# Peer retrieval step: decoding the top 16 indices on 16-bit pairs with a tree of additions, one-hot products from expert 51 on, gathers laid out anew

## What is computed

```python
q = (xt @ w_query).reshape(n, PEER_HEADS, 2, PEER_KEY_DIM).astype(jnp.float32)
s = jnp.einsum('nhpd,hpkd->nhpk', q, sub_keys.astype(jnp.float32))
s1, i1 = lax.top_k(s[:, :, 0], PEER_TOPK)
s2, i2 = lax.top_k(s[:, :, 1], PEER_TOPK)
cand = (s1[..., :, None] + s2[..., None, :]).reshape(n, PEER_HEADS, PEER_TOPK * PEER_TOPK)
cidx = (i1[..., :, None] * N_KEYS + i2[..., None, :]).reshape(n, PEER_HEADS, PEER_TOPK * PEER_TOPK)
top, pos = lax.top_k(cand, PEER_TOPK)
eidx = jnp.take_along_axis(cidx, pos, axis=-1)
gates = jax.nn.softmax(top, axis=-1).astype(x.dtype)
...
u = expert_u[eb]
act = jax.nn.gelu(jnp.einsum('nd,nhed->nhe', xb, u), approximate=False)
return jnp.einsum('nhe,nhed->nd', gb * act, expert_v[eb])
```

## Time and profile before

| what | value |
|---|---|
| median of 3 executions | 2011.06 us (2009.78 to 2013.45) |
| profiled execution, its time | 2013.25 us |
| profiled execution, its span | 2011.5 us |
| TensorE busy | 1832.2 us, 91% of the span |
| VectorE busy | 1564.5 us, 78% |
| GpSimd busy | 937.4 us, 47% |
| ScalarE busy | 651.3 us, 32% |
| chain that ended last | TensorE 64%, VectorE 26% |

### The profile page before, as it was taken

How to read it: one execution, slowest core, us unless ns; L and a number is a source line. 1 busy time by engine, 2 the same in 40 slices (tenths; PEclk the granted TensorE clock), 3 DMA queues, 4 the chain that set the end, 5 groups by cost and what they waited for, 6 DMA issues and landing times.

```text
span 2011.5 us, 29739 instructions
## 1 busy us (share of the span) xinstructions
PE 1832.2 (91%) x11606; PEld 1773.3 (88%) x11606; DVE 1564.5 (78%) x2742; ACT 651.3 (32%) x1029; POOL 937.4 (47%) x676
## 2 busy tenths in 40 slices
PE   3999687777979999999889999998999999999997
PEld 2999676665979999988889999997999999999996
DVE  3596877765348999999899999954688887888854
ACT  3444211122033333322324343432333333333332
POOL 2699899000000057788756656566144343434200
PEclk9999788875979999999999999999999999999998
DMA  6221100000552137877649999999899999999941
GB/s 186 64 83 53 48 1 1 1 1 6 170 160 75 64 131 268 280 255 262 227 157 299 303 300 302 301 308 410 311 349 397 356 359 345 353 359 354 343 172 34
DMA packets 192924, 424.86 MB, mean 211 GB/s; under 512 B 11204, under 2 KB 119264, under 8 KB 184585
## 3 DMA queue, kind: packets, MB, share of 16 engines
q1 hardware_dynamic: 155473, 287.99, 41.5%
q0 software_dynamic: 37312, 134.97, 19.2%
HBM read 361.28 MB, written 62.06 MB: 210 GB/s over the span
## 4 chain that ended last, share of the span: by engine, by line
PE 64%; DVE 26%; issue 3%; DMA 2%; ACT 2%; POOL 2%; DVEq 0%; ACTq 0%; POOLq 0%
PE psum L1137 29%; PE psum L1117 14%; PE psum L816 7%; PE psum L1105 4%; PE psum L811 3%; PE psum L900 2%; DMA rowg<-in_expert_u_rows,idx 2%; DVE sel L1868 1%; PE psum L958 1%; DVE cT L1555 1%; DVE eqa L1865 1%; DVE WR L1482 1%; DVE junk L1890 1%; DVE besti L1817 1%; DVE sring L1821 1%
## 5 line engine op out<-in xcount | busy, mean ns | idle before, releaser
L1117 PE MATMUL psum<-xT,WS 128*128 128x416 f32 x3072 | 607.5, 357 | 22.5 <-POOL WS L754 22.2
L1117 PEld LDWEIGHTS psum<-xT,WS 128*128 128x128 f32 x3072 | 580.0, 191 | 31.6 <-POOL WS L754 26.1
L1137 PE MATMUL psum<-AR,WS 128*128 128x416 f32 x3072 | 578.3, 350 | 2.6 <-DVE AR L1978 2.6
L1137 PEld LDWEIGHTS psum<-AR,WS 128*128 128x128 f32 x3072 | 573.5, 188 | 7.4 <-DVE AR L1978 3.0
L754 POOL TENSOR_TENSOR WS<-RAWP,WS 128x1024 fp32r<-128x1024 f32 x128 | 311.6, 2438 | 506.9 <-ACT WS L1381 505.9
L747 POOL DMA_INDIRECT rowg<-in_expert_v,idx x128 | 182.9, 1429 | 307.9 <-DVE acc L1903 297.9
L816 PE MATMUL psum<-xT,WR 128*128 128x280 f32 (+1 forms) x1968 | 263.7, 297 | 2.5 <-DVE xT L1500 2.5
L816 PEld LDWEIGHTS psum<-xT,WR 128*128 128x128 f32 x1968 | 260.7, 195 | 3.3 <-DVE xT L1500 3.2
L1391 ACT ACTIVATE WS<-RAWP 128x1024 fp32r<-128x1024 f32 x128 | 135.8, 1061 | 351.4 <-PE psum L1137 351.4
L1971 DVE TENSOR_TENSOR WS<-RAWP,WS 128x1024 fp32r<-128x1024 f32 x128 | 156.5, 1223 | 118.8 <-ACT WS L1391 118.8
L1418 ACT ACTIVATE actA<-psum 128x416 f32<-128x416 f32 x128 | 66.3, 518 | 448.4 <-PE psum L1117 417.7
(11 more groups left out here) (324 smaller groups left out, 1960.0 us busy)
## 6 DMA issues: line engine op xcount, KB each, us to landing
RAWP<-in_expert_u SPq DMA_DIRECT2D x64, 1024.0 KB, 6.9
RAWP<-in_expert_v SPq DMA_DIRECT2D x64, 1024.0 KB, 7.8
act_dram<-actA SPq DMA_DIRECT2D x128, 208.0 KB, 3.9
gate_dram<-gblk SPq DMA_DIRECT2D x13, 2048.0 KB, 11.9
Gt<-gate_dram SPq DMA_DIRECT2D x32, 832.0 KB, 7.0
act<-act_dram SPq DMA_DIRECT2D x64, 416.0 KB, 7.9
RAW<-in_w_in SPq DMA_DIRECT2D x8, 1024.0 KB, 6.4
RAW<-in_w_query SPq DMA_DIRECT2D x8, 1024.0 KB, 5.7
```

Source lines behind the costliest of these rows:

```text
L1117: last = mm(bank[e % 2][:, 0:TD], ws(e)[:, pw, kt * P:(kt + 1) * P], xT[:, px, kt, TSP:TPE], start=(kt == 0 and i == 0), stop=(kt == KT - ...
L1137: last = mm(bank[dt][:, 0:TD], ws(NK + e)[:, pw, dt * P:(dt + 1) * P], AR[:, e % 4, pa, :], start=(e == 0 and i == 0), stop=(e == NK - 1 a ...
```

## The change

Four things are done at once. The decode compares both halves of the position in one instruction, on bf16 values (`rowa`, which holds the row number 0 to 15 sixteen times each, against `topb`), multiplies in one instruction with `bestb`, which holds each index twice side by side, and adds up in four halving additions instead of two reduces. `level_two` has 9 `yield`s instead of 12, and at two of them a second dot is done, so 11 dots per tile and `L2DOTS` 44. The gates start behind expert 51 instead of 62, with all that is tied to them (46 for the exponential, 47 to 50 for the transposes, 112 for the first loads of the second loop). The gathers start behind low half 10 instead of 12 and come six to five experts instead of ten to nine; the last 24 come three to four experts, where the last 20 came three to one expert. The axpys start at expert 5 instead of 8.

```diff
--- before.py
+++ after.py
@@ -65,24 +65,26 @@
 NBAT = TD // OHB
 assert TD % ND == 0 and TD % GB == 0 and TD <= 512 and LASTP + TS == DB and DB <= P
 
-EXP_S_AT, EXP_D_AT = 10, 57
-PAIR_AT = {58 + i: 1 + i for i in range(ND)}
-GATE_AT = {62 + b: b for b in range(NBAT)}
-GSTORE_AT = {62 + 4 * blk + 5: blk for blk in range(NGB)}
-G2_AT = 121
-L2DOTS = 48
+GATE0 = 51
+EXP_S_AT, EXP_D_AT = 10, GATE0 - 5
+PAIR_AT = {GATE0 - 4 + i: 1 + i for i in range(ND)}
+GATE_AT = {GATE0 + b: b for b in range(NBAT)}
+GSTORE_AT = {GATE0 + 4 * blk + 5: blk for blk in range(NGB)}
+G2_AT = GATE0 + NBAT + 9
+L2DOTS = 44
 GATHER_AT = {}
 for _s in range(PAIRS):
     if _s < L2DOTS + 4:
-        _n = 12 + 9 * _s // 10
+        _n = 10 + 5 * _s // 6
     elif _s < L2DOTS + 8:
-        _n = 63 + _s - (L2DOTS + 4)
+        _n = GATE0 + 1 + _s - (L2DOTS + 4)
     elif _s < L2DOTS + 8 + NBAT:
-        _n = 67 + _s - (L2DOTS + 8)
+        _n = GATE0 + 5 + _s - (L2DOTS + 8)
     else:
-        _n = 119 + (_s - (L2DOTS + 8 + NBAT)) // 3
+        _n = GATE0 + NBAT + 5 + 3 * (_s - (L2DOTS + 8 + NBAT)) // 4
     GATHER_AT.setdefault(_n, []).append(_s)
-AX_START, AX_END = 8, 112
+assert max(GATHER_AT) < NK
+AX_START, AX_END = 5, 112
 
 
 class Steps:
@@ -264,15 +266,16 @@
         qT = place("qT", [P, 2, TPE], region="t")
         sring = place("sring", [P, 4, NTP, NK], region="t")
         cand = place("cand", [P, PH, TOPK, TOPK], region="k")
-        eqa = place("eqa", [P, PAIRS, TOPK], region="k")
-        sel = place("sel", [P, PAIRS, TOPK], region="k")
+        eqa = place("eqa", [P, 2 * PH, TOPK, TOPK], BF16, region="k")
+        sel = place("sel", [P, 2 * PH, TOPK, TOPK], BF16, region="k")
         used["t"] = max(used["t"], used["k"])
         best = place("best", [P, NTP, 2 * PH, TOPK], region="t")
         besti = place("besti", [P, NTP, 2 * PH, TOPK], U32, region="t")
-        bestf = place("bestf", [P, 2 * PH, TOPK], region="t")
+        bestb = place("bestb", [P, 2 * PH * TOPK, 2], BF16, region="t")
         topi = place("topi", [P, PAIRS], U32, region="t")
-        topa = place("topa", [P, 2, PAIRS], U32, region="t")
-        topf = place("topf", [P, 2, PAIRS], region="t")
+        topa = place("topa", [P, PH, 2, TOPK], U32, region="t")
+        topb = place("topb", [P, 2 * PH, TOPK], BF16, region="t")
+        rowa = place("rowa", [P, TOPK, TOPK], BF16, region="t")
         gmax = place("gmax", [P, PH], region="t")
         assert used["t"] <= room - D
 
@@ -1845,9 +1848,9 @@
                 n = PT[t][1]
                 sh = [n, PH, TOPK, TOPK]
                 bv = best[0:n, t].rearrange("p (h x) a -> p h x a", x=2)
-                fv = bestf[0:n].rearrange("p (h x) a -> p h x a", x=2)
                 cv, ev, lv = cand[0:n], eqa[0:n], sel[0:n]
-                op(dve.tensor_copy(bestf[0:n], besti[0:n, t]))
+                op(dve.tensor_copy(bestb[0:n], besti[0:n, t].rearrange("p c a -> p (c a)").unsqueeze(2).to_broadcast(
+                    [n, 2 * PH * TOPK, 2])))
                 chain(tt(cv, bv[:, :, 0, :].unsqueeze(3).to_broadcast(sh),
                          bv[:, :, 1, :].unsqueeze(2).to_broadcast(sh), ALU.add))
                 yield
@@ -1858,19 +1861,27 @@
                 hr = top16.rearrange("p (h r) -> p h r", h=PH)
                 chain(dve.tensor_copy(gmax[0:n], hr[:, :, 0]))
                 op(tt(hr, hr, gmax[0:n].unsqueeze(2).to_broadcast([n, PH, TOPK]), ALU.subtract), "top", t)
-                op(dve.tensor_scalar(topa[0:n, 0], topi[0:n], 4, None, ALU.logical_shift_right))
-                chain(dve.tensor_scalar(topa[0:n, 1], topi[0:n], 15, None, ALU.bitwise_and))
-                chain(dve.tensor_copy(topf[0:n], topa[0:n]))
-                for x in range(2):
-                    chain(tt(ev, iota[0:n, 0:TOPK].unsqueeze(1).to_broadcast([n, PAIRS, TOPK]),
-                             topf[0:n, x, :].unsqueeze(2).to_broadcast([n, PAIRS, TOPK]), ALU.is_equal))
-                    yield
-                    chain(tt(lv.rearrange("p (h r) a -> p h r a", h=PH),
-                             ev.rearrange("p (h r) a -> p h r a", h=PH),
-                             fv[:, :, x, :].unsqueeze(2).to_broadcast(sh), ALU.mult))
-                    yield
-                    chain(dve.tensor_reduce(pick[0:n, t, x, :], lv, AX.X, ALU.add))
-                    yield
+                ti = topi[0:n].rearrange("p (h r) -> p h r", h=PH)
+                op(dve.tensor_scalar(topa[0:n, :, 0, :], ti, 4, None, ALU.logical_shift_right))
+                chain(dve.tensor_scalar(topa[0:n, :, 1, :], ti, 15, None, ALU.bitwise_and))
+                chain(dve.tensor_copy(topb[0:n], topa[0:n].rearrange("p h x r -> p (h x) r")))
+                all_ = [n, 2 * PH, TOPK, TOPK]
+                chain(tt(ev, rowa[0:n].unsqueeze(1).to_broadcast(all_), topb[0:n].unsqueeze(2).to_broadcast(all_),
+                         ALU.is_equal))
+                yield
+
+                def by_two(m):
+                    return m.rearrange("p c a (r j) -> p (c a) r j", j=2)
+
+                chain(tt(by_two(lv), by_two(ev),
+                         bestb[0:n].unsqueeze(2).to_broadcast([n, 2 * PH * TOPK, TOPK // 2, 2]), ALU.mult))
+                yield
+                for m, a_, b_ in ((8, lv, ev), (4, ev, lv), (2, lv, ev)):
+                    chain(tt(b_[:, :, 0:m, :], a_[:, :, 0:m, :], a_[:, :, m:2 * m, :], ALU.add))
+                e4 = ev.rearrange("p (h x) a r -> p h x a r", x=2)
+                chain(tt(pick[0:n, t, 0:2, :].rearrange("p x (h r) -> p h x r", h=PH), e4[:, :, :, 0, :],
+                         e4[:, :, :, 1, :], ALU.add))
+                yield
 
             def weigh(t0, t1, n):
 
@@ -1905,14 +1916,17 @@
 
             dve.wait_ge(h2_done, 32)
             T.wait(dve, "score", 2 * PH - 1)
+            chain(dve.tensor_copy(rowa[:], iota[:, 0:TOPK].unsqueeze(2).to_broadcast([P, TOPK, TOPK])))
             for _ in level_two(0):
                 pass
             op(dve.scalar_tensor_tensor(idx[:], pick[:, 0, 0, :], float(NK), pick[:, 0, 1, :], ALU.mult, ALU.add),
                "idx")
             A.wait(dve, "xnP")
             for t in range(1, NTP):
-                for _ in level_two(t):
+                for i, _ in enumerate(level_two(t)):
                     next_dot()
+                    if i in (0, 8):
+                        next_dot()
                 if t == 1:
                     A.wait(dve, "gexp", 0)
                     weigh(0, 1, P)
```

## The result

The changed kernel takes 2020.96 us (median of six, 2017.68 to 2024.51) against 2012.38 for the kernel before (six, 2009.78 to 2013.51): ratio 1.0044, 95% interval 1.0032 to 1.0056. It is 9 us slower where 14 us faster was forecast. The profiled execution took 2020.71 us, with a span of 2019.0.

What follows compares the result with a forecast made beforehand. TensorE was taken to lose time to the late decode and to GpSimd waits in the tail. Gains of 1.5 + 11.5 = 13 us from 2011.06 give 1998, placed at 1997 us; 8-in-10 range 1984 to 2006.

Steps and rivals of the forecast that it cites:

- The bound: Before the second loop, TensorE loses time in two places: decode, 23.1 us late at the transposes, and tail, 12.2 us.
- The start: First tile: VectorE has the indices 8.0 us earlier; TensorE may miss 2 us before expert 11.
- The 16-bit instructions: Decode on VectorE: compare and multiply of 4096 16-bit elements take 2.3 us each, four additions 2.8 together.
- The slower rival: Decode: 16-bit instructions run at one element per f32 time, compare and multiply 4.4 us each; net 2028 us, chance 0.06.
- The waits inside the instructions: Decode tile: two waits of about 2 us go, additions meet GpSimd's subtraction once, 2.1 us; 1.8 us less per tile.
- the held instructions multiply: Rival, decode: multiply and additions each held 2.1 us per tile by GpSimd, 2.1 x 4 more; 2005 us, chance 0.16.
- The hand-over: From the fourth tile's end to the first transpose: 4.4 us, with 3 for the multiply and no wait for the exponential.
- The schedule: Schedule moved 11 experts (50.2 us) forward, VectorE gains 51.6: first transpose 21.6 us late instead of 23.1, 1.5 won.
- The ramp and the gates: Transposes, first one-hot batch and all 52 gate batches keep their distances and cost on TensorE: 0 us.
- The tail: Experts behind the gates: sparser gathers end GpSimd waits, gain 12.2 us, less 0.7 for queued stores: 11.5.
- the tail gives nothing: Rival: DMA at share 1.00, not the order of gathers, held the tail; about 2009 us, no-change chance 0.07.
- The second loop: Row additions from expert 5 and gelu behind expert 0 cost 0 us; under 1 if TensorE had to wait.

Runs made afterwards that it cites:

- e5: The change's new decode alone on the old schedule of the kernel before, with 12 dots per tile: 1994.3 us, ratio 0.9919 to the kernel before.
- e11: New decode on the old schedule, with the exponential behind expert 54 instead of 57: 1995.6 us, ratio 0.9928 to the kernel before.
- e13: Changed kernel with GpSimd subtracting only 16 of 1024 columns for experts 11 to 50 (output not right): 1990.5 us, ratio 0.9906 to the kernel before.
- e1: Changed kernel with four activation buffers instead of two, which also shifted AR by 2336 bytes: 2015.5 us, ratio 1.0019 to the kernel before.
- e2: Changed kernel with the second loop's five first loads spread behind experts 112 to 121 instead of all behind 112: 2016.4 us, ratio 1.0013.
- e7: Kernel before with four activation buffers instead of two, tables shifted by 2336 bytes: 2015.1 us, ratio 1.0032 to the unedited kernel before.
- e3: Changed kernel with two 16-bit reduces in place of the four halving additions: 2037.2 us, ratio 1.0116 to the kernel before.
- e9: Changed kernel with four activation buffers and AR and the second loop's other tables 4096 bytes further: 2012.6 us, ratio 1.0006 to the kernel before.

## Why the prediction was wrong

*The bound.* Right: what TensorE loses ahead of the second loop, it loses in the decode and in the tail.

*The start.* Right. The indices stand 45.2 us behind the loop start, 8.1 earlier than before, where 8.0 was worked out, and TensorE's miss before expert 11 is 2.24 us, where it said 2.

*The 16-bit instructions.* Right: 2.29 us for compare and multiply. The slower rival's mechanism (4.4 us each) did not occur.

*The waits inside the instructions: the first step that failed.* It said that "the additions come one dot later and should meet the subtraction once, 2.1 us". In most tiles they meet it twice, and the tiles took 198.8 us, where the steps of the prediction leave 190.9 (945.5 less 709.4 and 45.2): 7.9 us more. The third addition is held in three of the four tiles, 7.0 us; `cand` is held once, 2.9 us; the conversions to pairs, held once instead of twice, give 1.5 back. The working let the chain of additions meet the subtraction once, and missed that a chain has a new chance to be held at each of its gaps: four short additions are more exposed than one reduce. The rival called "the held instructions multiply" had this mechanism and, with 8.4 us, about the right size for the tiles; but it named the multiply, which is never held in the change, and so the size is in part luck.

*The hand-over: the same cause.* 4.4 us forecast, 8.9 measured: the multiply took 5.1, above the longest row before (4.64), and `iotab` 2.6 instead of 0.22 (before, GpSimd was at its gathers then, its next subtraction began at 989.10). In four kernels in which this multiply met a row of subtractions it ended 0.55 us behind the last one, however long that took: 4.64 before, 5.09 in the change, 7.01 in e5, 9.97 in e11. Its price is what is left of the row, and not a time of its own. With these two terms the first transpose is 12.4 us later than forecast; e13 shows that the subtraction is behind it.

The Trainium skill, SBUF — State Buffer, section Who interferes with whom, says that a VectorE instruction with two SBUF inputs contends with a GpSimd instruction that reads SBUF, that casts can contend too, and that the reduce never does. The section that the prediction cites speaks of the 2-port modes; it is this one that covers the two-input additions. The trace agrees: additions and casts are held (2.75 instead of 0.42 us, 3.11 instead of 0.29), reduces aren't (2.28 to 2.29). The hold costs here up to one whole subtraction (2.4 us) per gap, or several.

*The schedule.* The sum was right in form: the schedule moved TensorE's date by 50.2 us, and VectorE had to gain as much. But with a forecast of 51.7 it had 1.5 us of reserve for terms that were off by 12. e5, the same decode on the old dates, won the 16 us.

*The ramp and the gates.* Right to within 1 us.

*The tail: the second step that failed.* GpSimd's wait went as worked out. Behind it stood ScalarE's wait for the activation store, 30.5 us in the trace of before, which the prediction leaves out. It kept back 0.7 us "for stores that queue behind these loads", a size that it took from no row; behind a burst the gelu is held up to 12.8 us, and with two buffers 3 to 6 us of it reach TensorE. The rival "the tail gives nothing" names this outcome, but by a DMA share of 1.00, which fell. e1 (clean), e2 (one of two stalls gone) and e7 (no gain in the kernel before) show it. That the loads now meet fewer gathers, the reason given for 112 instead of 121, did not keep the stores from being late.

*The second loop.* 1.5 us longer. The tables lie where they did, and e2, with the same places, takes 578.3 us as before. The difference is in the clock: in the loop's first 20 us the mean granted clock is 0.91 and TensorE does 98 matmuls, against 1.00 and 106 before and in e2, so part of that stretch ran at the lower of its two levels (1.2 instead of 2.4 GHz). The same 2.6 us of idle time stand ahead of it in all three; what brings the lower clock is not shown.

The two steps are 12.5 and 10.2 us; the other stages (-2.5, -0.8, -0.4, +1.5) take 2.2 back, which leaves the 20.4 by which the sum missed.

## What to carry to other kernels

Price a rewrite by the gaps that it has beside an engine that can hold it, not only by its elements: in a chain of short instructions each gap is a chance to lose a whole foreign instruction. Make the faster work first, and move the dates of the engine that waits only as far as a trace of it allows: the same decode on the old dates won 16 us. When a limit is taken away, look in the trace for waits that lay beside it, also those that cost nothing yet: the late stores were there before, with 30.5 us.

## What the runs showed of the hardware

- A two-input VectorE instruction can be shut out by several GpSimd instructions in a row: 9.97 us beside 9.36 us of four subtractions (e11). It then needs its own time less 0.12 to 0.14 us behind the last of them.
- A reduce of 2048 bf16 elements that lie 16 apart takes 4.2 us (e3), the f32 one of neighbours 2.28.
- The place in SBUF of a loop's tables, TensorE's moving one among them, changed 3072 matmuls from 579.8 to 584.4 us, with no wait in either (e1, e9), and from 578.3 to 582.8 (before, e7).
